# The pre-norm factors of the first two tiles applied behind the transposition, by blocks of channels, and loaded to all partitions for the rest

## The reference, cut to what matters

```python
def rmsnorm(x, g):
    xf = x.astype(jnp.float32)
    y = xf * lax.rsqrt(jnp.mean(xf * xf, axis=-1, keepdims=True) + EPS)
    return (y * g.astype(jnp.float32)).astype(x.dtype)

hp = rmsnorm(xp, pre_norm_g[i])      # i = 0: a factor per row, then a factor g per channel
p = h @ w_in                         # 1024 -> 3072, mixer A
a, g_glu, z = jnp.split(p, 3, axis=-1)
c = a * jax.nn.sigmoid(g_glu)
```

## Time and profile before

| | us |
|---|---|
| median of 3 runs | 2300.79 |
| lowest, highest | 2300.56, 2303.32 |
| the profiled execution | 2300.46 |
| its span | 2298.7 |

### The profile page before, as it was taken

One profiled execution on the slowest core, in us unless ns is written; L12 is line 12 of the kernel. 1 busy time (PEld: TensorE's weight loads), 2 busy tenths in 40 slices (PEclk: granted clock), 3 DMA queues, 4 the chain that ended last, 5 costly groups with the idle time before them and its releaser, 6 DMA issues.

```text
span 2298.7 us, 30297 instructions
## 1 busy us (share of the span) xinstructions
PE 2258.9 (98%) x12048; PEld 1968.5 (86%) x12048; DVE 1641.8 (71%) x2043; ACT 923.6 (40%) x1389; POOL 253.7 (11%) x422
## 2 busy tenths in 40 slices
PE   8999999999999999999998999999999999998998
PEld 7788899999888887888886888877789999997886
DVE  5599989997577988989888937742286666766221
ACT  6422222223353225666664125531135655565110
POOL 3100000101221101000000011211010010100000
PEclk9999999999999999999999999999999999999999
DMA  4323333333434313333336246342213333336330
GB/s 171 115 92 110 110 120 128 107 104 123 151 138 166 130 61 110 98 106 120 121 117 228 102 142 215 138 165 80 83 60 91 98 99 100 95 95 249 110 101 28
DMA packets 126077, 274.66 MB, mean 119 GB/s; under 512 B 17137, under 2 KB 53617, under 8 KB 124274
## 3 DMA queue, kind: packets, MB, share of 16 engines
q1 hardware_dynamic: 102530, 194.35, 25.8%
q0 software_dynamic: 23408, 78.38, 9.8%
HBM read 194.30 MB, written 78.75 MB: 119 GB/s over the span
## 4 chain that ended last, share of the span: by engine, by line
PE 93%; DMA 2%; DVE 2%; ACT 1%; issue 1%; POOL 0%; SPq 0%; DVEq 0%; ACTq 0%
PE PS L2079 30%; PE PS L2081 29%; PE PS L2080 29%; PE PS L2297 2%; PE PS L2090 1%; PE PS L2167 1%; PE PS L2145 1%; DMA yb<-y_scratch 1%; DMA rawb<-wb_out_in 0%; DMA raw<-wa_in_in 0%; DMA s_scratch<-m 0%; DMA st<-s_scratch 0%; PE PS L2154 0%; DVE xn L1483 0%; PE PS L2300 0%
## 5 line engine op out<-in xcount | busy, mean ns | idle before, releaser
L1515 DVE SCALAR_TENSOR_TENSOR acc<-cp,cw,acc 128x513 f32<-128x513 f32 (+3 forms) x464 | 360.3, 777 | 13.5
L2079 PE MATMUL PS<-HAh,Wh 128*128 128x512 f32 (+3 forms) x968 | 343.3, 355 | 0.0
L2081 PE MATMUL PS<-HAh,Wl 128*128 128x512 f32 (+3 forms) x968 | 341.2, 353 | 0.0
L2080 PE MATMUL PS<-HAl,Wh 128*128 128x512 f32 (+3 forms) x968 | 341.2, 352 | 0.0
L2079 PE MATMUL PS<-Wbh,s7h 128*128 128x512 f32 (+1 forms) x544 | 213.7, 393 | 13.4 <-DVE Wbl L1473 11.9
L2079 PE MATMUL PS<-Vh,HBh 128*128 128x512 f32 (+1 forms) x544 | 212.4, 390 | 0.1
L2080 PE MATMUL PS<-Wbl,s7h 128*128 128x512 f32 (+1 forms) x544 | 211.9, 390 | 0.0
L2081 PE MATMUL PS<-Wbh,s7l 128*128 128x512 f32 (+1 forms) x544 | 211.8, 389 | 0.0
L2080 PE MATMUL PS<-Vl,HBh 128*128 128x512 f32 (+1 forms) x544 | 211.8, 389 | 0.0
L2081 PE MATMUL PS<-Vh,HBl 128*128 128x512 f32 (+1 forms) x544 | 211.7, 389 | 0.0
L2081 PEld LDWEIGHTS PS<-HAh,Wl 128*128 128x128 f32 x968 | 182.7, 189 | 14.9
(11 more groups left out here) (211 smaller groups left out, 5034.9 us busy)
## 6 DMA issues: line engine op xcount, KB each, us to landing
raw<-wa_in_in SPq DMA_DIRECT2D x48, 512.0 KB, 3.6
rawv<-wb_v_in SPq DMA_DIRECT2D x64, 256.0 KB, 4.7
QWr<-wb_uz_in SPq DMA_DIRECT2D x64, 256.0 KB, 2.6
v_scratch<-vb POOLq DMA_DIRECT2D x64, 256.0 KB, 2.6
vt<-v_scratch SPq DMA_DIRECT2D x32, 512.0 KB, 3.9
s_scratch<-m POOLq DMA_DIRECT2D x32, 512.0 KB, 4.1
rawb<-wb_out_in SPq DMA_DIRECT2D x28, 512.0 KB, 7.8
st<-s_scratch SPq DMA_DIRECT2D x13, 1024.0 KB, 4.9
```

The costliest lines, as they stand in the source:

```text
L1515: return nc.vector.scalar_tensor_tensor(out=out, in0=src, scalar=w, in1=first, op0=ALU.mult, op1=ALU.add)
L2079: nc.tensor.matmul(out, wh, xh, start=start, stop=False, skip_group_check=seeded)
L2080: nc.tensor.matmul(out, wh, xl, start=False, stop=False, skip_group_check=seeded)
L2081: return nc.tensor.matmul(out, wl, xh, start=False, stop=stop, skip_group_check=seeded)
```

## The change

Tiles 0 and 1 are scaled by their row factors alone, in a VectorE instruction with one tensor input (`tensor_scalar`). Behind the transposition, where a channel is a partition, `n1_high` makes 8 ScalarE copies of 128 by 128 with the block's column of factors as scale, and `n1_low` makes 8 VectorE instructions (PSUM times column, minus high part). The columns come with the constants (`con`, 129 to 137 columns wide). For the tiles from 2 on, `gpre` is now a DMA of 512 KB that reads the same 4 KB row for each partition, issued behind x tile 2. The factors' matmuls, the row of ones and the copy of the banks are gone. The low part of weights 0 goes from VectorE to GpSimd, behind the factors of tiles 0 and 1.

Three orders change besides. ScalarE squares only tiles 0 and 1 ahead, does tiles 0 and 1, squares 2 and 3, and from then on squares the tile two further on, not three. TensorE transposes tiles 0 and 1 ahead of the first product, tile 2 behind step 3 and tile 3 behind step 4 of its first half, and tile 4 behind step 3 of its second half. SyncE issues x tile 1, weights 0, x tile 2, `gpre`.

```diff
-            sp.dma_start(gpre[0:1, :], pre_g[0:1, :]).then_inc(n1_g, 16)
-            for t in range(1, 3):
-                x_load(t)
+            x_load(1)
             a_load(0)
+            x_load(2)
+            sp.dma_start(gpre[:, :], pre_g[0:1, :].to_broadcast([P, D])).then_inc(n1_g, 16)
...
             for t in range(9):
                 n1_rsqrt(t)
+                if t == 1:
+                    a_low(0)
...
             def n1_high(t):
...
+                if t < 2:
+                    act.wait_ge(ld_con, 16)
+                    for k in range(KD):
+                        act.wait_ge(n1_tr, KD * t + 4 * (k // 4 + 1))
+                        nc.scalar.activation(in_half(HAh[0], t)[:, k, :], src[:, k, :], ACT.Copy, scale=gcol[k])\
+                            .then_inc(n1_hi, 1)
+                    return
...
-            for t in range(3):
+            for t in range(2):
                 n1_square(t)
             a_high(0)
-            for t in range(8):
+            for t in range(2):
                 n1_high(t)
-                if t + 3 < 9:
-                    n1_square(t + 3)
+            for t in range(2, 4):
+                n1_square(t)
+            for t in range(2, 8):
+                n1_high(t)
+                if t + 2 < 9:
+                    n1_square(t + 2)
                 if t in (2, 4):
                     a_high(t // 2)
-                if t == 0:
-                    act.wait_ge(n1_g, 17)
-                    act.wait_ge(n1_sc, 2)
-                    nc.scalar.activation(gpre[:, :], banks(2), ACT.Copy).then_inc(n1_g, 1)
...
             def n1_scale(t):
...
+                if t < 2:
+
+                    nc.vector.tensor_scalar(xn[s][0:n, :], xt[x_slot(t)][0:n, :], rn1[0:n, t:t + 1], None, ALU.mult)\
+                        .then_inc(n1_sc, 1)
+                    return
...
             def n1_low(t):
...
+                if t < 2:
+                    for k in range(KD):
+                        dve.wait_ge(n1_hi, KD * t + 4 * (k // 4 + 1))
+                        nc.vector.scalar_tensor_tensor(out=in_half(HAl[0], t)[:, k, :], in0=src[:, k, :],
+                                                       scalar=gcol[k], in1=in_half(HAh[0], t)[:, k, :].bitcast(fp32),
+                                                       op0=ALU.mult, op1=ALU.subtract).then_inc(n1_lo, 1)
+                    return
...
             n1_scale(0)
             n1_scale(1)
-            a_low(0)
-            for t in range(8):
+            dve.wait_ge(ld_con, 16)
+            for t in range(2):
+                n1_low(t)
+            for t in range(2, 4):
+                n1_scale(t)
+            for t in range(2, 8):
                 n1_low(t)
                 if t + 2 < 9:
                     n1_scale(t + 2)
...
-                        if half == 0 and k == 2:
-                            n1_transpose(3)
-                        if half == 0 and k == 6:
+                        if half == 0 and k in (3, 4):
+                            n1_transpose(k - 1)
+                        if half == 1 and k == 3:
                             n1_transpose(4)
```

More of the change, by code:

```diff
@@ L126, in build @@
         g = Region(base, top)
-        con = g("con", [P, P + 1])
+        con = g("con", [P, P + 1 + KD])
         ident, one = con[:, 0:P], con[:, P:P + 1]
+        gcol = [con[:, P + 1 + k:P + 2 + k] for k in range(KD)]
         par = g("par", [P, NPAR])
@@ L132, in build @@
         half_neg = g("half_neg", [P, NTILES])
-        ones_row = g("ones_row", [1, P])
         bst = g("bst", [P, 2, 6])
@@ L386, in x_slot, with n1_after @@
             return t if t < 6 else t % 2
+        def n1_after(t):
+            return KD * (t + 1) if t < 2 else 2 * KD + t - 1
         def x_use(t):
@@ L645, in o_load_y @@
                     if h == 0:
-                        sp.wait_ge(n1_tr, NTILES)
+                        sp.wait_ge(n1_tr, n1_after(NTILES - 1))
                 if t >= TILES[h][0] + 3:
@@ L913, in a_low @@
                 pool.wait_ge(a_hi, n + 1)
-                pool.wait_ge(a_lo, n)
+                if n > 0:
+                    pool.wait_ge(a_lo, n)
                 nc.gpsimd.tensor_tensor(kp(Wl[n % 3]), kp(raw[n % 3]), kp(Wh[n % 3]).bitcast(fp32), ALU.subtract)\
@@ L1074, in n1_square @@
                 if t >= 8:
-                    act.wait_ge(n1_tr, t - 1)
+                    act.wait_ge(n1_tr, n1_after(t - 2))
                 n = rows(t)
@@ L1477, in n1_scale @@
                 dve.wait_ge(n1_r, t + 1)
-                if t >= 2:
-                    dve.wait_ge(n1_tr, t - 1)
-                dve.wait_ge(n1_g, 17 if t < 2 else 18)
-                factors = banks(2) if t < 2 else gpre
+                if t < 2:
+                    nc.vector.tensor_scalar(xn[s][0:n, :], xt[x_slot(t)][0:n, :], rn1[0:n, t:t + 1], None, ALU.mult)\
+                        .then_inc(n1_sc, 1)
+                    return
+                dve.wait_ge(n1_tr, n1_after(t - 2))
+                dve.wait_ge(n1_g, 16)
                 nc.vector.scalar_tensor_tensor(out=xn[s][0:n, :], in0=xt[x_slot(t)][0:n, :], scalar=rn1[0:n, t:t + 1],
-                                               in1=factors[0:n, :], op0=ALU.mult, op1=ALU.mult).then_inc(n1_sc, 1)
+                                               in1=gpre[0:n, :], op0=ALU.mult, op1=ALU.mult).then_inc(n1_sc, 1)
             def n1_low(t):
-                dve.wait_ge(n1_hi, t + 1)
                 b = 4 if t < 8 and t % 2 else 6
@@ L1490, in n1_low @@
                 src = banks(b).rearrange("p (k n) -> p k n", k=KD)[:, :, 0:rows(t)]
+                if t < 2:
[5 more added lines that the diff above has]
+                    return
+                dve.wait_ge(n1_hi, n1_after(t))
                 split_low(in_half(HAl[h], t), src, in_half(HAh[h], t), n1_lo)
@@ L2085, in n1_transpose @@
                 pe.wait_ge(n1_sc, t + 1)
-                if t >= 8 or t >= 2:
-                    pe.wait_ge(n1_lo, t if t >= 8 else t - 1)
+                if t >= 2:
+                    pe.wait_ge(n1_lo, n1_after(t - 1 if t >= 8 else t - 2))
                 b = 4 if t < 8 and t % 2 else 6
@@ L2091, in n1_transpose @@
                                                ident[0:n, 0:n])
-                last.then_inc(n1_tr, 1)
+                    if t < 2:
+                        last.then_inc(n1_tr, 1)
+                if t >= 2:
+                    last.then_inc(n1_tr, 1)
             def a_first_chunk():
                 for half in range(2):
-                    pe.wait_ge(n1_lo, 2 * (half + 1))
+                    pe.wait_ge(n1_lo, n1_after(2 * half + 1))
                     cols = slice(256 * half, 256 * (half + 1))
@@ L2117, in a_chunk @@
                 if n == 0 and c == 1:
-                    pe.wait_ge(n1_lo, 8)
-                if p == 2:
-                    pe.wait_ge(n1_g, 18)
+                    pe.wait_ge(n1_lo, n1_after(7))
                 if n == UNITS_A and c == 0:
-                    pe.wait_ge(n1_lo, NTILES)
+                    pe.wait_ge(n1_lo, n1_after(NTILES - 1))
                 if (n, c) == (0, 0):
@@ L2424, in b_last_tile @@
                 last.then_inc(o_main, 1)
-            pe.wait_ge(c_neg, 2)
-            pe.wait_ge(n1_g, 16)
-            for c in range(2):
-                last = nc.tensor.matmul(PS[:, 2 + c, :], ones_row[:, :], gpre[0:1, 512 * c:512 * (c + 1)],
-                                        start=True, stop=True)
-            last.then_inc(n1_g, 1)
+            pe.wait_ge(c_neg, 1)
             pe.wait_ge(ld_con, 16)
-            for t in range(3):
+            for t in range(2):
                 n1_transpose(t)
@@ L2493 @@
         "s_bias": np.asarray(b_s_bias)[0].reshape(1, GROUPS * P),
-        "consts": np.concatenate([np.eye(P, dtype=np.float32), np.ones((P, 1), np.float32)], axis=1),
+        "consts": np.concatenate([np.eye(P, dtype=np.float32), np.ones((P, 1), np.float32),
+                                  columns(pre_norm_g[0])], axis=1),
     }
```

5 lines of the change are left out of this document (2 added, 3 removed).

## The result

| | before | after |
|---|---|---|
| median, us (9 runs each) | 2300.56 | 2305.97 |
| lowest, highest, us | 2298.11, 2806.45 | 2303.43, 2308.62 |
| the profiled execution, us | 2300.46 | 2307.19 |
| its span, us | 2298.7 | 2305.4 |

The 2806.45 is a single run of the kernel before; the next highest is 2303.32, and without it the median is the same to 0.01 us. The changed kernel is slower: ratio 1.0024, 95% interval 1.0015 to 1.0033. The whole interval is above 1, and the 0.2% that the prediction set as its bound lies inside it. The forecast was 2304.8.

What follows compares the result with a forecast made beforehand. TensorE, busy 2258.9 of 2298.7 us, was taken as the bound, with the second product's start deciding. Earlier start -1.2, late second half +1.0 and second wait +3.2 were put at +4.2; forecast 2304.8 us, range 2301.0 to 2308.8.

Steps and rivals of the forecast that it cites:

- The first product, 15.0: TensorE's first product was to begin at 15.0 us, 2.8 earlier than 17.83, only 1.2 of it real.
- The estimate of 0.29: Spacing in us of ScalarE's new small blocks, the middle between bounds of 0.20 and 0.387.
- The wait ahead of the second half, 3.8 and 25.15: TensorE waits some 3.8 us for tile 3's low part; first product's second half begins at 25.15, not 24.15: +1.0.
- The second half, 7.83 us to the second product: First product's second half to second product: 7.83 us, before 4.64, with a second TensorE wait of 2.5: +3.2.
- The sum, +4.2: Second product begins at 33.0 us instead of 28.79, and the whole execution ends 4.2 us later.
- the fall of the clock in the new wait: Rival: TensorE's clock falls in the wait ahead of the second half, making +5.5 to +7; chance 0.20.
- A shift of that moment should come out one for one: Any shift of the second product's start, 28.79 us before, reaches the end of the program in full.
- The load hidden: The 512 KB load of `gpre` ends at about 11 to 12 us, 4 ahead of scale 2, costing nothing.
- GpSimd's low part hidden: Low part of weights 0 on GpSimd takes 2.40 us, about 9.1 to 11.5, needed at 15: no cost.
- The two-column price: Rival: ScalarE's small blocks are 0.387 us apart, first product at 16.5, sum +5.7; chance 0.17.
- The waits came: Answers the rival that TensorE's new waits stay away, leaving -1.2 us, or -4.0 at the faster side; chance 0.10.
- swallowed: Rival: the wait before 76.79 us takes back the shift, up to 4.2 us, leaving 0; chance 0.08.

Runs made afterwards that it cites:

- load_later: Changed kernel with the load of `gpre` issued behind x tiles 3 and 4; median 2305.66 us, ratio 1.0028 to the kernel before.
- after_again: The changed kernel as it is, profiled a second time; one run, 2305.07 us.
- wide_copies: Changed kernel with the small blocks of tiles 0 and 1 made as one instruction per tile on either engine, channel factors left out; 2306.95 us, ratio 1.0028.
- pe_order_before: Changed kernel with TensorE's transpositions where they stood in the kernel before; 2305.74 us, ratio 1.0019 to the kernel before.
- x2_before_weights: Changed kernel with x tile 2 issued ahead of weights 0 on SyncE, as before; one run, 2308.48 us.
- before_squares_late: Kernel before with ScalarE's squares from 4 on one high part later; 2303.09 us, ratio 1.0010 to the kernel before.

## Why the prediction was right, step by step

**The first product, 15.0: it was 14.69.** The blocks on ScalarE were 0.249 apart, not 0.29, so they took 0.65 us less. Of this 0.3 arrived: VectorE's sixteen, 0.26 apart from 10.31 on, then set the pace. The estimate of 0.29 was the mis-sized term; its upper end came from rows with two columns that read SBUF (yb, 569 us), while these blocks read PSUM. That this is the reason is argued; no run here made the same block from both. The rows above have the same copy of 1024 elements from both, though: from SBUF (weights 1, 21.29) the next instruction starts 0.95 behind it, from PSUM (tile 2's high part, 19.33) 0.92. The Trainium skill ("Perfetto Trace Analysis", section "Optimizing Scalar/DVE Operations") gives ScalarE's access overhead as about 93 ns on SBUF and 51 on PSUM; the difference of 0.04 us is as large as that between 0.29 and 0.249, and near the 0.03 of those two rows.

**The wait ahead of the second half, 3.8 and 25.15: it was 2.68 and 24.86.** The releaser and the order that makes it (square 4, weights 1, then the high part of tile 3; scale 4 ahead of tile 3's low part) were as said. The size of the wait was off, because TensorE was through at 22.2 and not at 21.4: that 21.4 comes out only with the upper clock from step 4 on, and the clock rose during transposition 3 (matmuls of 256 columns are 0.21 us apart ahead of it and 0.12 behind it). What counts, the start of the second half, was off by 0.3, all of it from the first product.

**The second half, 7.83 us to the second product: it was 7.84** (24.86 to 32.70), with a wait of 2.03 for scale 6, where 2.5 had been forecast. The term was right.

**The sum, +4.2: at the second product it was +3.9 in one profile of the changed kernel and +5.4 in the other.** Two things were not in the sum. The first is the landing of x tile 1. The prediction took it as 6.7, and the square that waits for it starts anywhere up to 8.2. In the kernel before this costs nothing, since the factors' matmuls and the queue on ScalarE cover it: with the square at 8.19 the second product came at 28.72. In the changed kernel the first product stands 7.84 to 7.93 behind the square: in load_later, with the square at 7.94, it came at 15.80 and the second half at 25.87, both 1.0 to 1.1 later than in the changed kernel's first profile. The second is the fall of the clock in the new wait, the rival that was given 0.20; it came in three of the five profiles that have both of the change's orders (after_again, load_later, wide_copies), so that chance was small. In after_again the landing cost nothing in the end: its first product was 0.67 later, but the clock rose by transposition 2, which the prediction had priced at 0.9 to come back, and the second half was 0.05 earlier. All of its extra 1.5 us lies behind that, with the clock low.

**"A shift of that moment should come out one for one": nearly so up to 98 us, and not beyond.** In the changed kernel the shift is 3.91 at the second product, 4.15 at transposition 13 (80.94) and 4.13 at the next wait (98.01), and 6.28 at 620 us. Between them lies a second fall of the clock. The window from 100 to 101 us, of the changed kernel and then of the one before (columns as in the earlier trace rows):

```profile
100.00:101.00 1.00, 1.00 (x4) 0.82 (x3) 1.00 (x3) 1.00 (x2) 0.00 (x0) 0.50 0.00 0
```

```profile
100.00:101.00 1.00, 1.00 (x10) 0.59 (x9) 0.94 (x2) 0.52 (x2) 0.00 (x0) 1.00 0.46 184
```

In after_again the shift is 5.43, 5.39 and 4.50 at the same places and 4.8 at 619 us: there the clock was low for 3.4 us behind that transposition, before for 6.8. What TensorE waits is carried through; how long the clock stays low behind the waits near 80 and 98 us differs, and moves a single execution by 1 to 2 us either way. The median is +5.4, 1.2 above the sum; the two profiled executions ended at +6.7 and +4.6.

**The load hidden, GpSimd's low part hidden, weights 1 and 2 in time:** all as said, shown by load_later and by the rows above. The load of `gpre` was issued at 3.1 us and landed at 10.7, scale 2 started at 15.33; the low part of weights 1 ends at 27.59 for the second product at 32.70.

**The rivals.** The two-column price (0.387) is refuted by 0.249. The waits came, and were not swallowed: ahead of transposition 13 TensorE waits 4.51 us, before 4.23. The choice among "within" and "slower" was near even, 0.52 to 0.43, and the measured 0.24% falls on the slower side of the bound, with its interval on both. The range of 2301.0 to 2308.8 holds the time. That the time came within 1.2 us of the point of 2304.8 is in part luck: in the first profile the second product was 0.3 us below the sum and the end 2.5 above it, in the other 1.2 and 0.4 above.

**What stays open.** How much of the median's excess over the sum is the landing of x tile 1 and how much the clock; one or two profiles of each kernel can't tell. Why x tile 1 lands between 6.7 and 8.2 was not found either.

## What to carry to other kernels

Work that starts earlier is worth nothing if the instructions that follow it stand late in another engine's queue: recompute for every engine what stands between two dependent instructions. Two orders that are each late must be mended together; either alone gave back 0.8 to 1.2 us at the second product and nothing in the median. And look for the wait that both kernels share: two weights' loads issued ahead of blocked ones, the first of them 6.3 us earlier, gained 5.6 us, as much as the whole change had lost.

## What the runs showed of the hardware

- A small GpSimd instruction on 128 x 1, 0.22 us by itself, took 1.24 to 1.32 us when VectorE ran a scale with two SBUF inputs, and ended 0.1 us behind it. The other way round, a scale that takes 1.28 us lasted 3.40 from 25.28 on, beside GpSimd's low part of 25.21 to 27.59. The Trainium skill ("SBUF — State Buffer", section "Who interferes with whom") says that a VectorE instruction with two SBUF inputs and a GpSimd instruction that reads SBUF shut each other out for a whole instruction; the trace agrees.
- A copy of 128 x 128 from PSUM with one column as scale: 0.249 us apart on ScalarE. A VectorE scale with one tensor input and a column, 1024 elements, took 0.75 us in the changed kernel (tile 0, 6.46), against 1.28 with two inputs.
- The granted clock fell behind idle stretches of 3.24, 3.26 and 3.27 us ahead of the first product's second half and not behind 2.68, 2.71 and 2.72. In after_again an earlier rise of the clock made the wait longer, and the fall came with it. Near 98 us it fell behind waits of 2.00 to 2.52 us in four kernels (after, pe_order_before, x2_before_weights, before_squares_late), and in none with 1.35 to 1.81 there; ahead of transposition 13 it fell behind all of them, the shortest 2.52 to 2.60 us; and in before_squares_late it fell at 17.05, after an idle stretch of 1.86 us ahead of transposition 2. So over these places of the program no one length of wait parts the falls from the rest.
- At the start of the program the granted clock of the windows doesn't show the lower level: in the changed kernel it reads 1.00 from 14 to 20 us, where matmuls of 256 columns are 0.21 us apart, as they are in after_again's window of 0.50. There the level is read from the spacing.
